# A router block and an experts block: logits turned first, lists copied on ScalarE, one gather and one fold moved across the block boundary

## The chip, the core and the metric

The kernel runs on one core of one Trainium2 chip. The time is the device time of that core in microseconds (us). TensorE, VectorE (DVE), ScalarE (ACT), GpSimd (POOL) and SyncE (SP) run their own instruction streams and meet by semaphores. SyncE computes nothing here; it issues DMAs, which 16 DMA engines carry out.

## What is computed

The reference runs two networks one after the other on a tensor x of 1024 tokens by 1024 features, all in fp32: a first block (modulated mixer of windowed attention and mLSTM, then a mixture of experts) and a second block of two layers (pooling and spatial gate, then dilated attention and short convolutions). The change lies in the mixture of experts and in a weight product that the second block's first layer wants ready:

```python
def expert_choice_ffn(h, w_router, w_gate, w_up, w_down):      # 16 experts, 1024 tokens
    cap = CAPACITY * N // N_EXPERTS                            # 128 tokens for each expert
    aff = jax.nn.softmax((h @ w_router).astype(f32), -1)
    gate, idx = lax.top_k(jnp.swapaxes(aff, 1, 2), cap)
    xg = h[bidx, idx]
    g = jnp.einsum('becd,edf->becf', xg, w_gate)
    u = jnp.einsum('becd,edf->becf', xg, w_up)
    y = jnp.einsum('becf,efd->becd', jax.nn.silu(g) * u, w_down) * gate[..., None]
    return jnp.zeros_like(h).at[bidx, idx].add(y)

# second block, even layer: z = h @ w_in; a is z's first quarter
pooled = trailing means of a minus a, in 4 groups of 256 features
mixed = jnp.einsum('bsgc,gcd->bsgd', pooled, pool_w)
```

The pooling runs over tokens and `pool_w` over features, so the kernel multiplies each group's 1024x256 slice of `w_in` with that group's `pool_w` beforehand. This product is called a fold. Three of the four groups are folded beside the router, each in two parts of 512 rows (parts P0 to P5), the fourth at the end of the experts.

## The kernel before

The program is a chain of blocks. A block holds one stream for each engine, and ends with a meeting of all of them. Semaphores of a block are taken from one of two sets in turn, and GpSimd clears the older set between blocks; a few semaphores are kept across blocks (`gathered`, `fold_stored`, `next_up_loaded`).

**`phase_router` (L2240 to L2538).** The products of x with the router's weights are in PSUM already (`router_z`). Its steps:

- TensorE first turns the shift column into rows (8 transposes, L2389), then the logits (2 transposes, L2394), which wait for ScalarE's copy of the products (L2453). ScalarE copies the shift rows (L2457) and then runs the exponential (L2459). VectorE does the rest of the softmax (L2490 to L2504).
- TensorE turns the affinities (L2400); VectorE copies them and finds the 128 best of each expert in 16 rounds of `max`, `max_index` and `match_replace` (L2516 to L2520), for both halves of the tokens at once.
- VectorE copies the lists: positions as floats, and both lists in reverse order (L2522 to L2524). TensorE turns all four (L2424, L2425), and VectorE merges the two halves into `slot_gate` and `slot_token` (L2528 to L2537).
- Beside it, in the order of `ORDER`, TensorE turns eight row blocks of x (R0 to R7, `turn_rows`), ScalarE scales them out of PSUM, GpSimd adds the shift (L2346), and SyncE stores them to `h2_rows` in memory (L2314). Between them stand the six fold parts: `turn_part` and `mix_part` on TensorE, `take_part` and `give_part` on ScalarE, `store_fold` on SyncE (L2319). ScalarE also casts the gate and up weights of expert 0 to their high parts (L2451) and GpSimd subtracts for their low parts (L2351).
- SyncE's last steps: it waits for all six mixes, loads `raw_up[1]` (L2333), whose buffer lies over fold part 0 and `w_mix`, and stores part 5.

**`phase_experts` (L2540 to L2898).** For each of 16 experts, every fp32 product is three matmuls on a high and a low part. GpSimd gathers the expert's 128 rows from `h2_rows` by `slot_token` (L2639), TensorE turns them (`turn`, L2676), then come `gate` (L2686 to L2690), `up` (L2699 to L2702), the turning of their product (L2710) and `down` (L2736 to L2741), one expert later. ScalarE casts weights and x to high parts (L2793, L2797), VectorE subtracts for the low parts (L2857, L2861), ScalarE weighs the result and GpSimd scatters it with an add (L2646). Raw weights have two buffers each. SyncE works through one list in order: it waits for both first gathers (L2614) and for the stored folds, loads `raw_down[1]`, the last fold's operands (L2615 to L2617), and then for each expert `load` (L2610), each released by the matmuls that have used the buffer's last contents.

Of the kernel before, what the change touches and what calls it, by code (L numbers as in the profile page):

```python
# [187 lines left out]
def build_program(nc, A, out):  # L188
    with ExitStack() as ctx:
# [2049 lines left out]

        def phase_router(router_z, first_turn):  # L2240
# [37 lines left out]
            first_fold_stored = sem("fold_first_stored")  # L2278
            top_done = sem("route_top_done")
            top_turned = sem("route_top_turned")  # L2280
            raw_loaded = sem("route_raw_loaded")
# [7 lines left out]
            turned_w = Arena(nc, ring_at + 2 * KT * P * 4 * 2)("fold_turned", [P, 2, 2, HALF])  # L2289
            fold_mem = Arena(nc, exp_raw_at["down", 1])  # L2290
            w_parts = [first_part] + [fold_mem(f"fold_part{g}", [P, KT, 2 * P]) for g in range(1, FOLDED)]
            assert fold_mem.at <= exp_mem.at
# [3 lines left out]

            def part_rows(i):
                return slice(i % 2 * (KT // 2), (i % 2 + 1) * (KT // 2))

            with nc.psum_tensor("route_fold", [P, 4, HALF], F32) as fold, nc.Block() as block:  # L2300
# [6 lines left out]
                @block.sync  # L2307
                def _(sp):
                    def load_part(g):
                        sp.dma_start(w_parts[g][:], even_w[:, :, g * 2 * P:(g + 1) * 2 * P]).then_inc(fold_loaded[g], 16)  # L2310

                    def store_rows(j):
                        sp.wait_ge(rows_shifted, 2 * j + 2)
                        sp.dma_start(h2_rows[j * P:(j + 1) * P, :], rows[j % SETS][:].rearrange("p a n -> p (a n)")).then_inc(stored[j % SETS], 16)  # L2314

                    def store_fold(i):
                        sp.wait_ge(fold_out, i + 1)
                        g = i // 2
                        sp.dma_start(fold_w[:, part_rows(i), g * 2 * P:(g + 1) * 2 * P], w_parts[g][:, part_rows(i), :]).then_inc(fold_stored if g else first_fold_stored, 16)  # L2319

                    load_part(1)
                    load_part(2)
                    for j in range(4):
                        store_rows(j)
                    sp.dma_start(exp_raw["down", 0][:], exp_src["down"][:, 0]).then_inc(raw_loaded, 16)
                    store_fold(0)
                    for j in range(4, BLOCKS):
                        store_rows(j)
                    for i in range(1, 5):
                        store_fold(i)  # L2330
                    sp.wait_ge(fold_mixed, 2 * FOLDED)
                    sp.wait_ge(first_fold_stored, 32)
                    sp.dma_start(exp_raw["up", 1][:], exp_src["up"][:, 1]).then_inc(next_up_loaded, 16)  # L2333
                    store_fold(5)
                    for u in range(SETS):
                        sp.wait_ge(stored[u], 16 * len(range(u, BLOCKS, SETS)))
                    sp.wait_ge(raw_loaded, 16)

                @block.gpsimd
                def _(pool):  # L2340
# [6 lines left out]
                    for n, w in enumerate(("gate", "up")):  # L2347
                        pool.wait_ge(hi_done, n + 1)
                        for part in range(4):
                            k = slice(part * EXP_SHAPES[w][1] // 4, (part + 1) * EXP_SHAPES[w][1] // 4)  # L2350
                            pool.tensor_tensor(exp_lo[w, 0][:, k], exp_raw[w, 0][:, k], exp_hi[w][:, k].bitcast(F32), ALU.subtract)  # L2351

                @block.tensor
                def _(pe):
# [32 lines left out]

                    for kt in range(KT):
# [3 lines left out]
                    pe.wait_ge(products_out, 1)  # L2392
                    for b in range(2):
                        ins = pe.transpose(logits[:, b * P:(b + 1) * P], products[:, b * P:(b + 1) * P], ident)  # L2394
                    ins.then_inc(logits_done, 1)
# [23 lines left out]
                    mix_part(5)  # L2419
                    pe.wait_ge(fold_out, 5)  # L2420
                    pe.wait_ge(top_done, 1)
# [7 lines left out]
                def _(act):  # L2429
# [51 lines left out]
                    give_part(5)  # L2481

                @block.vector
                def _(dve):
# [37 lines left out]
                    step(dve.tensor_copy(top_at_f[:], top_at[:]))  # L2522
                    step(dve.tensor_copy(top_back[:], top[:, ::-1]))
                    step(dve.tensor_copy(top_at_back[:], top_at[:, ::-1]))  # L2524
                    step.wait()
                    dve.sem_inc(top_done, 1)
# [10 lines left out]
                    step(dve.tensor_tensor(slot_token[:], apart[:], second[:, 1, :], ALU.add))  # L2537


        def phase_experts(first_rows, first_rows_loaded):  # L2540
# [4 lines left out]
            xg = mem("x_gathered", [P, 2, D])  # L2545
# [11 lines left out]
            gathered = [phases.keep(f"exp_gathered{u}") for u in range(2)]  # L2557
# [11 lines left out]
            half_down = sem("exp_half_down")  # L2569
            rows_copied = sem("exp_rows_copied")  # L2570
# [32 lines left out]
            with nc.psum_tensor("exp_turn", [P, 2, HALF], F32) as p_x, nc.psum_tensor("exp_gate", [P, 2, HALF], F32) as p_gu, \  # L2603
# [3 lines left out]
                def _(sp):  # L2607
# [4 lines left out]
                    for u in range(2):  # L2612
                        sp.wait_ge(gathered[u], 16)
# [21 lines left out]
                def _(pool):  # L2635
# [13 lines left out]
                    for e in range(4):  # L2649
# [20 lines left out]
                def _(pe):  # L2670
# [55 lines left out]
                    def down(e, halves_=range(2)):  # L2726
                        if 0 in halves_:
                            pe.wait_ge(f_hi_done, e + 1)
                            if e:
                                pe.wait_ge(y_out, e)  # L2730
                        for half in halves_:
# [11 lines left out]

                    turn(0)
# [39 lines left out]
                def _(act):  # L2784
# [26 lines left out]
                    hi("down", 0)  # L2811
                    hi_x(0)
# [2324 lines left out]
```

## Time and profile before

| | us |
|---|---|
| median of 3 runs | 3230.51 |
| lowest, highest | 3228.77, 3232.57 |
| the profiled execution | 3233.75 |
| its span in the trace | 3231.9 |
| TensorE busy (PE) | 3097.2 (96%) |
| VectorE, ScalarE, GpSimd busy | 1700.8, 1453.7, 1702.4 |
| DMA | 388.11 MB, 120 GB/s over the span |

In the trace the router's block lies from about 781 to 830 us and the experts' from there to about 1135. A row of a timeline gives start and duration in us, the engine, the line of the kernel, the operation, output<-input by the program's names, their shapes and the number of instructions merged; in brackets stands the idle time of the engine before it and what ended that. A row with xN above 1 runs from its start for its whole duration. `PEclk` is the granted clock of TensorE as a share of 2.4 GHz.

### The profile page before, as it was taken

To read this page: it belongs to the slowest core of one execution; us is meant where nothing else is said; L and a number is where in the kernel's file an instruction comes from. 1 tells how busy PE (TensorE), PEld (TensorE's weight loads), DVE (VectorE), ACT (ScalarE), POOL (GpSimd) and SP (SyncE) were. 2 spreads that over 40 slices of the span, in tenths; PEclk is the share of its full clock that TensorE was granted. 3 is DMA by queue.
4 is the path that set the end of the run, shared out by engine and by line. 5 is a ranking of instruction groups with operands and counts; after the bars stand their busy time and mean duration, and the time that the engine had idled before them with its cause. 6 is when DMAs were issued, how large, how long until landed. Compare 5 with 4: busy or idle time off the path is not lost. (4 is left out here: it accounts for less than half of the span.)

```text
span 3231.9 us, 43925 instructions
## 1 busy us (share of the span) xinstructions
PE 3097.2 (96%) x16268; PEld 2574.3 (80%) x16268; DVE 1700.8 (53%) x2449; ACT 1453.7 (45%) x2460; POOL 1702.4 (53%) x1112
## 2 busy tenths in 40 slices
PE   6989999979899989999999999999999999999998
PEld 4777887857688868788888788888888888888777
DVE  5366633855799776623523744444444444367545
ACT  5156322724577743333301545455455455333443
POOL 2331323044321249877643656556556556688886
PEclk8999999989899989999999999999999999999999
DMA  8230212175899952222422111111111111244543
GB/s 298 56 87 21 57 40 68 51 253 167 324 400 394 357 165 79 78 85 63 172 91 74 40 54 45 46 56 43 46 56 43 47 56 43 89 147 163 182 162 106
DMA packets 340339, 388.11 MB, mean 120 GB/s; under 512 B 29239, under 2 KB 297435, under 8 KB 333860
## 3 DMA queue, kind: packets, MB, share of 16 engines
q1 hardware_dynamic: 328222, 344.39, 31.7%
q0 software_dynamic: 4896, 16.78, 2.1%
q10 hardware_dynamic: 7014, 24.17, 1.9%
q8 instruction: 131, 2.15, 0.3%
q14 instruction: 76, 0.62, 0.1%
HBM read 313.73 MB, written 68.16 MB: 118 GB/s over the span
## 5 line engine op out<-in xcount | busy, mean ns | idle before, releaser
L3011 POOL TENSOR_TENSOR quarter_lo<-quarter_w_sums,quarter_hi 128x512 fp32r<-128x512 f32 x325 | 467.6, 1446 | 247.9 <-ACT quarter_hi L3005 245.1
L3011 POOL TENSOR_TENSOR quarter_lo<-quarter_raw,quarter_hi 128x512 fp32r<-128x512 f32 x244 | 356.2, 1460 | 277.7 <-ACT quarter_hi L3005 270.8
L3101 PE MATMUL odd_z<-odd_t_hi,quarter_hi 128*128 128x512 f32 x876 | 362.3, 414 | 4.0 <-POOL quarter_lo L3011 2.5
L3005 ACT CAST quarter_hi<-quarter_w_sums 128x512 fp32r<-128x512 f32 x325 | 202.4, 623 | 360.6 <-PE first_z L3103 172.8
L3101 PE MATMUL first_z<-odd_t_hi,quarter_hi 128*128 128x512 f32 x868 | 359.1, 414 | 4.1 <-ACT last_rows L3115 2.3
L3103 PE MATMUL odd_z<-odd_t_hi,quarter_lo 128*128 128x512 f32 x876 | 343.3, 392 | 0.0
L3102 PE MATMUL odd_z<-odd_t_lo,quarter_hi 128*128 128x512 f32 x876 | 341.9, 390 | 0.0
L3103 PE MATMUL first_z<-odd_t_hi,quarter_lo 128*128 128x512 f32 x868 | 340.4, 392 | 0.0
L3102 PE MATMUL first_z<-odd_t_lo,quarter_hi 128*128 128x512 f32 x868 | 338.8, 390 | 0.0
L3005 ACT CAST quarter_hi<-quarter_raw 128x512 fp32r<-128x512 f32 x244 | 151.6, 622 | 120.7 <-PE first_z L3103 55.8
L276 POOL TENSOR_TENSOR w_hi<-w_raw,zero_col 128x1024 fp32r<-128x1024 f32 x25 | 49.6, 1984 | 290.9 <-DMA w_raw<-in_w_in 98.1
L3101 PEld LDWEIGHTS odd_z<-odd_t_hi,quarter_hi 128*128 128x128 f32 x876 | 165.2, 189 | 35.9 <-POOL quarter_lo L3011 3.4
L3103 PEld LDWEIGHTS odd_z<-odd_t_hi,quarter_lo 128*128 128x128 f32 x876 | 164.6, 188 | 36.2
L3103 PEld LDWEIGHTS first_z<-odd_t_hi,quarter_lo 128*128 128x128 f32 x868 | 163.2, 188 | 35.9
L3101 PEld LDWEIGHTS first_z<-odd_t_hi,quarter_hi 128*128 128x128 f32 x868 | 163.7, 189 | 34.9 <-issue 5.5
L3102 PEld LDWEIGHTS odd_z<-odd_t_lo,quarter_hi 128*128 128x128 f32 x876 | 165.5, 189 | 30.0
L3102 PEld LDWEIGHTS first_z<-odd_t_lo,quarter_hi 128*128 128x128 f32 x868 | 164.0, 189 | 29.7
L4769 DVE SCALAR_TENSOR_TENSOR dil_biased<-const,odd_aux 128x128 f32<-128x128 f32 (+1 forms) x192 | 78.0, 406 | 192.7 <-PE odd_aux L4280 122.6
L3115 ACT ACTIVATE dil_set<-odd_z 128x512 f32<-128x512 f32 x112 | 90.8, 810 | 174.8 <-PE odd_z L3103 174.8
L3115 ACT ACTIVATE dil_set<-first_z 128x512 f32<-128x512 f32 x108 | 88.3, 817 | 166.6 <-PE first_z L3103 166.6
L4789 DVE COPY dil_p_t<-odd_aux 128x128 f32<-128x128 f32 (+1 forms) x192 | 67.7, 353 | 172.1 <-PE odd_aux L4297 150.7
L3018 POOL TENSOR_TENSOR quarter_w_sums<-quarter_raw 128x512 f32<-128x512 f32 x82 | 119.4, 1456 | 29.2 <-POOL quarter_lo L3011 13.4
(720 smaller groups left out, 7799.0 us busy)
## 6 DMA issues: line engine op xcount, KB each, us to landing
quarter_raw<-in_odd_w_in SPq DMA_DIRECT2D x224, 256.0 KB, 3.4
raw_gate<-in_w_gate SPq DMA_DIRECT2D x16, 2048.0 KB, 15.5
raw_up<-in_w_up SPq DMA_DIRECT2D x16, 2048.0 KB, 15.0
raw_down<-in_w_down SPq DMA_DIRECT2D x16, 2048.0 KB, 14.9
quarter_raw<-in_even_w_in SPq DMA_DIRECT2D x64, 256.0 KB, 3.2
start_w_mod<-in_w_mod SPq DMA_DIRECT2D x11, 1024.0 KB, 10.8
w_raw<-in_w_in SPq DMA_DIRECT2D x16, 512.0 KB, 3.8
mix_w_early<-in_w_mod SPq DMA_DIRECT2D x8, 1024.0 KB, 12.0
```

The lines of the kernel that those rows point to most:

```text
L276: pool.tensor_tensor(w_hi[:, u], w_raw[:, u], zero_col[:, 0:1].to_broadcast([P, KT * P]).rearrange("p (k n) -> p k n", k=KT), ALU.add).the ...
L3005: act.copy(self.home(n)[0][:], self.source(m, i)).then_inc(self.hi_done, 1)
L3011: pool.tensor_tensor(lo[:], self.source(m, i), hi[:].bitcast(F32), ALU.subtract).then_inc(self.split, 1)
L3018: pool.tensor_tensor(sums[:, 0], a21, a22, ALU.add).then_inc(self.added, 1)
L3101: pe.matmul(to, w_hi[:, kt], t_hi[:, kt], start=(begins and kt == 0), stop=False, skip_group_check=True)
L3102: pe.matmul(to, w_hi[:, kt], t_lo[:, kt], start=False, stop=False, skip_group_check=True)
L3103: ins = pe.matmul(to, w_lo[:, kt], t_hi[:, kt], start=False, stop=(kt == KT // 2 - 1), skip_group_check=True)
L3115: act.activation(to[t][half], self.bank(m, i, banks, to), ACT.Copy, scale=scale).then_inc(self.copied, 1)
L4769: dve.scalar_tensor_tensor(out=biased[:, u % 2, 0:w], in0=dist, scalar=cst("slopes")[:, g * C_SLOTS + h:g * C_SLOTS + h + 1], in1=score[:, ...
L4789: dve.tensor_copy(p_t[:, u % 2, 0:w], turned[:, 0:w]).then_inc(free, 1)
```

## The change

The logits are turned ahead of the shift. The three copies of the lists go from VectorE to ScalarE, with a semaphore `top_found` from VectorE and a count of three on `top_done`. GpSimd issues the gather for expert 0 at the end of the router's block, behind its subtractions, a wait for all stored rows and a new semaphore `slots_known`; the tile `x_gathered` and its semaphores are therefore made outside both phases. The mix of fold part 5 leaves the router's block and is done by TensorE at the start of the experts' block, into `p_y`, ahead of `turn(0)`; ScalarE copies it out behind the cast of down(0), and SyncE stores it. The load of `raw_up[1]` moves with it: SyncE issues it behind gather 0 and that mix, and stores part 5 next. Nothing of the work is left out.

```diff
@@ -2237,6 +2237,18 @@
+        xg_mem = Arena(nc, exp_mem.at)
+        xg = xg_mem("x_gathered", [P, 2, D])
+        xg_end = xg_mem.at
+        gathered = [phases.keep(f"exp_gathered{u}") for u in range(2)]
+        turned_w = Arena(nc, ring_at + 2 * KT * P * 4 * 2)("fold_turned", [P, 2, 2, HALF])
+        fold_parts_mem = Arena(nc, exp_raw_at["down", 1])
+        w_parts = [first_part] + [fold_parts_mem(f"fold_part{g}", [P, KT, 2 * P]) for g in range(1, FOLDED)]
+        assert fold_parts_mem.at <= exp_mem.at
...
+        def part_rows(i):
+            return slice(i % 2 * (KT // 2), (i % 2 + 1) * (KT // 2))
...
         def phase_router(router_z, first_turn):
@@ -2276,8 +2288,10 @@
             first_fold_stored = sem("fold_first_stored")
+            top_found = sem("route_top_found")
             top_done = sem("route_top_done")
             top_turned = sem("route_top_turned")
+            slots_known = sem("route_slots_known")
             raw_loaded = sem("route_raw_loaded")
@@ -2286,16 +2300,9 @@
             wide = [P, BLOCKS, N_EXPERTS]
-            turned_w = Arena(nc, ring_at + 2 * KT * P * 4 * 2)("fold_turned", [P, 2, 2, HALF])
-            fold_mem = Arena(nc, exp_raw_at["down", 1])
-            w_parts = [first_part] + [fold_mem(f"fold_part{g}", [P, KT, 2 * P]) for g in range(1, FOLDED)]
-            assert fold_mem.at <= exp_mem.at
             ORDER = "R0 R1 P0 P1 R2 R3 R4 P2 R5 R6 R7 P3 P4 P5".split()
...
             FOLD_AT = [ORDER.index(f"P{i}") for i in range(2 * FOLDED)]
...
-            def part_rows(i):
-                return slice(i % 2 * (KT // 2), (i % 2 + 1) * (KT // 2))
@@ -2326,12 +2333,9 @@
                         store_rows(j)
-                    for i in range(1, 5):
+                    for i in range(1, 2 * FOLDED - 1):
                         store_fold(i)
-                    sp.wait_ge(fold_mixed, 2 * FOLDED)
                     sp.wait_ge(first_fold_stored, 32)
-                    sp.dma_start(exp_raw["up", 1][:], exp_src["up"][:, 1]).then_inc(next_up_loaded, 16)
-                    store_fold(5)
                     for u in range(SETS):
@@ -2349,6 +2353,11 @@
                             pool.tensor_tensor(exp_lo[w, 0][:, k], exp_raw[w, 0][:, k], exp_hi[w][:, k].bitcast(F32), ALU.subtract)
+                    for u in range(SETS):
+                        pool.wait_ge(stored[u], 16 * len(range(u, BLOCKS, SETS)))
+                    pool.wait_ge(slots_known, 1)
+                    pool.indirect_dma_start(xg[:, 0, :], None, h2_rows, bass.IndirectOffsetOnAxis(ap=slot_token[:, 0:1], axis=0),
+                                            bounds_check=SEQ - 1).then_inc(gathered[0], 16)
@@ -2385,14 +2394,14 @@
+                    pe.wait_ge(products_out, 1)
+                    for b in range(2):
+                        ins = pe.transpose(logits[:, b * P:(b + 1) * P], products[:, b * P:(b + 1) * P], ident)
+                    ins.then_inc(logits_done, 1)
                     for kt in range(KT):
...
                             ins.then_inc(shift_turned, 1)
-                    pe.wait_ge(products_out, 1)
-                    for b in range(2):
-                        ins = pe.transpose(logits[:, b * P:(b + 1) * P], products[:, b * P:(b + 1) * P], ident)
-                    ins.then_inc(logits_done, 1)
                     turn_rows(0)
@@ -2416,9 +2425,8 @@
                     mix_part(4)
-                    mix_part(5)
                     pe.wait_ge(fold_out, 5)
-                    pe.wait_ge(top_done, 1)
+                    pe.wait_ge(top_done, 3)
@@ -2478,7 +2486,10 @@
                     give_part(4)
-                    give_part(5)
+                    act.wait_ge(top_found, 1)
+                    act.copy(top_back[:], top[:, ::-1]).then_inc(top_done, 1)
+                    act.copy(top_at_f[:], top_at[:]).then_inc(top_done, 1)
+                    act.copy(top_at_back[:], top_at[:, ::-1]).then_inc(top_done, 1)
@@ -2519,11 +2530,7 @@
                         step.wait()
-                    step(dve.tensor_copy(top_at_f[:], top_at[:]))
-                    step(dve.tensor_copy(top_back[:], top[:, ::-1]))
-                    step(dve.tensor_copy(top_at_back[:], top_at[:, ::-1]))
-                    step.wait()
-                    dve.sem_inc(top_done, 1)
+                    dve.sem_inc(top_found, 1)
                     dve.wait_ge(top_turned, 1)
@@ -2535,6 +2542,8 @@
                     step(dve.tensor_tensor(slot_token[:], apart[:], second[:, 1, :], ALU.add))
+                    step.wait()
+                    dve.sem_inc(slots_known, 1)
@@ -2542,7 +2551,7 @@
             FK, shapes, raw, w_hi_, w_lo_ = FFK, EXP_SHAPES, exp_raw, exp_hi, exp_lo
-            xg = mem("x_gathered", [P, 2, D])
+            mem.at = xg_end
             x_hi = mem("x_hi", [P, 2, KT, P], F32R)
@@ -2554,7 +2563,6 @@
             used = {w: sem(f"exp_{w}_used") for w in shapes}
-            gathered = [phases.keep(f"exp_gathered{u}") for u in range(2)]
             turned = sem("exp_turned")
@@ -2567,6 +2575,8 @@
             half_down = sem("exp_half_down")
+            part_mixed = sem("fold_rest_mixed")
+            part_out = sem("fold_rest_out")
             rows_copied = sem("exp_rows_copied")
@@ -2609,8 +2619,12 @@
-                    for u in range(2):
-                        sp.wait_ge(gathered[u], 16)
+                    sp.wait_ge(gathered[0], 16)
+                    sp.wait_ge(part_mixed, 1)
+                    sp.dma_start(raw["up", 1][:], exp_src["up"][:, 1]).then_inc(next_up_loaded, 16)
+                    sp.wait_ge(part_out, 1)
+                    sp.dma_start(fold_w[:, part_rows(5), 4 * P:6 * P], w_parts[2][:, part_rows(5), :]).then_inc(fold_stored, 16)
+                    sp.wait_ge(gathered[1], 16)
                     sp.wait_ge(fold_stored, 16 * 2 * (FOLDED - 1))
@@ -2646,7 +2660,7 @@
-                    for e in range(4):
+                    for e in range(1, 4):
                         gather(e)
@@ -2728,6 +2742,8 @@
                                 pe.wait_ge(y_out, e)
+                            else:
+                                pe.wait_ge(part_out, 1)
                         for half in halves_:
@@ -2741,6 +2757,11 @@
+                    for kt in range(KT // 2):
+                        for c in range(2):
+                            ins = pe.matmul(p_y[:, kt // 2, kt % 2 * 2 * P:(kt % 2 + 1) * 2 * P], turned_w[:, 1, c, kt * P:(kt + 1) * P],
+                                            w_mix[:, 4 + c, :], start=(c == 0), stop=(c == 1))
+                    ins.then_inc(part_mixed, 1)
                     turn(0)
@@ -2809,6 +2830,8 @@
                     hi("down", 0)
+                    act.wait_ge(part_mixed, 1)
+                    act.copy(w_parts[2][:, part_rows(5), :].rearrange("p (a k) n -> p a (k n)", a=2), p_y[:]).then_inc(part_out, 1)
                     hi_x(0)
```

## Rows read from the trace of the kernel before

**Rows 1.** Stretches: us, busy us (instructions) of PE, PEld, DVE, ACT, POOL; PEclk, DMA share, GB/s

```profile
821.00:831.00 10.00, 2.03 (x9) 1.78 (x8) 6.97 (x17) 1.85 (x2) 5.37 (x3) 0.66 0.81 266
831.00:842.00 11.00, 5.08 (x15) 4.08 (x16) 5.72 (x3) 5.15 (x4) 4.82 (x3) 0.50 0.55 159
842.00:890.00 48.00, 46.90 (x217) 38.88 (x216) 35.95 (x21) 32.21 (x23) 6.56 (x3) 0.97 0.99 377
890.00:1110.00 220.00, 220.00 (x1044) 183.67 (x1043) 199.62 (x111) 173.66 (x124) 48.83 (x24) 1.00 1.02 396
```

**Rows 2.** Timeline of SyncE's DMA queue: loads around the boundary, and two gate loads

```profile
821.21 0.35 SPq L2333 DMA_DIRECT2D raw_up<-in_w_up  x1
...
838.82 0.35 SPq L2615 DMA_DIRECT2D raw_down<-in_w_down  x1
...
839.70 3.71 SPq L2617 DMA_DIRECT2D fold_last_mix<-in_even_pool_w  x1
...
860.56 0.33 SPq L2610 DMA_DIRECT2D raw_gate<-in_w_gate  x1
...
1073.33 0.33 SPq L2610 DMA_DIRECT2D raw_gate<-in_w_gate  x1
```

**Rows 3.** DMA issues at 822, 860 and 1073 us; last number: us to landing

```profile
fold_w<-fold_part SPq DMA_DIRECT2D x1, 512.0 KB, 10.3
...
raw_gate<-in_w_gate SPq DMA_DIRECT2D x1, 2048.0 KB, 8.1
...
raw_gate<-in_w_gate SPq DMA_DIRECT2D x1, 2048.0 KB, 21.0
```

**Rows 4.** Timelines of VectorE and TensorE late in the experts: down(14)

```profile
1108.25 4.49 DVE L2857 TENSOR_TENSOR lo_down<-raw_down,hi_down 128x2048 fp32r<-128x2048 f32 x2 [0.40 <-ACT hi_down L2793]
...
1115.41 0.39 PE L2736 MATMUL exp_y<-hi_down,f_hi 128*128 128x512 f32 x1
```

**Rows 5.** Timeline of VectorE: the lists' copies and the merge

```profile
822.85 3.60 DVE L2522 CAST aff_top_at_f<-aff_top_at 48x128 f32<-48x128 uint32 x1
...
826.51 0.21 DVE L2524 CAST aff_top_at_back<-aff_top_at 48x128 f32<-48x128 uint32 x1
828.82 0.17 DVE L2528 COPY aff_second<-route_fold 128x16 f32<-128x16 f32 x1 [2.10 <-PE route_fold L2425]
...
829.69 0.18 DVE L2537 TENSOR_TENSOR slot_token<-aff_apart,aff_second 128x16 uint32<-128x16 f32 x1
```

**Rows 6.** Timeline of GpSimd: last subtractions, gathers 0 and 2

```profile
817.11 9.26 POOL L2351 TENSOR_TENSOR lo_up<-raw_up,hi_up 128x1024 fp32r<-128x1024 f32 x4
831.19 1.24 POOL L2639 DMA_INDIRECT x_gathered<-h_rows,slot_token  x1 [4.82 <-issue]
...
838.56 1.01 POOL L2639 DMA_INDIRECT x_gathered<-h_rows,slot_token  x1 [3.26 <-PE exp_turn L2676]
```

**Rows 7.** Timeline of TensorE: start of the router's block, folds 4 and 5, expert 0

```profile
781.38 1.94 PE L2389 MATMUL route_fold<-const,mod 128*128 128x128 f32 x8 [0.58 <-PEq L2054]
783.12 0.46 PE L2394 MATMUL route_fold<-const,aff_products 128*128 128x128 f32 x2
...
814.10 7.07 PE L2384 MATMUL route_fold<-fold_w_mix,fold_turned 128*128 128x256 f32 x32
...
835.82 1.97 PE L2676 MATMUL exp_turn<-const,x_gathered 128*128 128x128 f32 x8 [7.04 <-DMA x_gathered<-h_rows,slot_token]
838.89 0.80 PE L2686 MATMUL exp_gate<-hi_gate,x_hi 128*128 128x512 f32 x1 [1.10 <-ACT x_hi L2797]
...
845.37 2.00 PE L2690 MATMUL exp_gate<-hi_gate,x_lo 128*128 128x512 f32 x8
847.20 0.39 PE L2699 MATMUL exp_gate<-hi_up,x_hi 128*128 128x512 f32 x1
```

**Rows 8.** Timeline of ScalarE at the start of the router's block

```profile
783.15 1.06 ACT L2457 COPY h_shift_rows<-route_fold 128x512 f32<-128x512 f32 x2
784.98 0.31 ACT L2459 ACTIVATE aff<-aff 128x128 f32<-128x128 f32 x1 [0.77 <-DVE aff L2496]
```

## The prediction

> **What bounds the kernel now.** I read the page first, then the stretch tables, and then each engine's timeline around the edited code, because the edit touches 60 us of a 3232 us span. Two facts come out of the tables. From 890 to 1110 us, inside the experts, TensorE is busy 220.00 of 220.00 us, and the DMA engines are busy too, at a share of 1.02 and 396 GB/s [rows 1]. So two resources are full at once, and the question is which of them ends an expert.
>
> The queue of SyncE answers it. The gate load of expert 3 is issued at 860.56 and that of expert 15 at 1073.33 [rows 2]; both are released by TensorE, so TensorE needs (1073.33 - 860.56)/12 = 17.73 us for an expert. The first of them lands 8.1 us after its issue, the second 21.0 us after [rows 3]. They land at 868.7 and 1094.3, so the DMA engines need 18.8 us for an expert. The transfers fall behind TensorE by about 1.1 us with every expert, and TensorE does not notice it, because each buffer is asked for early. What is left of that cover at the end can be read off: the low part of down(14) is ready at 1108.25 + 4.49 = 1112.74, and the first matmul that needs its second half runs at 1115.41 [rows 4]. The cover is 2.7 us.
>
> Ahead of the experts lies the serial chain that the change shortens. The lists of the router end on VectorE with a cast of a 48x128 tile that took 3.60 us, while the same cast took 0.21 us right behind it [rows 5]. GpSimd's four subtractions run from 817.11 to 826.37 [rows 6], and the long cast ends at 826.45, just behind them: VectorE waited for GpSimd's SBUF access. Then come TensorE's turning of the lists (VectorE idle 2.10 us), 1.05 us of small steps to 829.87, the block's end, GpSimd's gather at 831.19, and TensorE's first transposes for expert 0 at 835.82 [rows 5 to 7]. The first gate projection starts at 838.89, behind a wait of 1.10 us for the high part of x, and runs at half clock: TensorE's granted clock was 0.50 from 831 to 842 (1.2 GHz) and 1.00 later [rows 1, 7].
>
> **Part 1, logits turned first.** TensorE enters the block at 781.38 and turned the shift for 1.94 us before it came to the logits at 783.12 [rows 7]. Now only ScalarE's short copy of the products lies ahead of them; I put their start at 781.8. VectorE's chain to the exponential would be about 1.1 us earlier. But ScalarE has the two copies of the shift rows (783.15, 1.06 us for both) ahead of the exponential (784.98) [rows 8], and those now wait for transposes that start 0.9 us later. These end at about 782.3 + 1.6 to 1.9, and the exponential comes at about 784.5 to 784.8. I take a gain of 0.35 us; bounds 0 and 1.1.
>
> **Part 2, lists copied by ScalarE.** ScalarE is free then: its last copy of a fold part leaves the block, and a 128x128 exponential took 0.31 us [rows 8]. Three copies back to back take about 0.75 us (bounds 0.6 and 1.2). They replace 826.72 - 822.85 = 3.87 us on VectorE [rows 5]. Gain 3.1 us. Chain: index search done at 822.47, lists at 823.3, turned at 825.2 (about 1.9 us as now), small steps to 826.3. Two of these steps read two SBUF tiles; GpSimd is then at its last subtraction (to about 826.0), so up to 0.3 us is added: slots known at about 826.55 instead of 829.9.
> The Trainium skill says the same of the wait: the "GPSIMD Engine Reference", section Key points, has GpSimd sharing its SBUF interfaces with VectorE, in conflict with a two-port mode or with two SBUF inputs. By it the cast goes, and the 0.3 us of the two-input steps stays; the trace agrees as to the cast (3.60 against 0.21 us).
>
> **Part 3, first gather in the router's block.** From a semaphore to the start of a gather GpSimd took 0.77 us (TensorE's turn ends at 837.79, the gather starts at 838.56), and the instruction lasts 1.24 us [rows 6, 7]. So it starts at 827.3 and ends at 828.55. All engines now wait for GpSimd at the block's end: the experts' block opens at about 829.05 where it did at about 830.16. The rows arrive 4.63 us after the start (835.82 - 831.19 [rows 6, 7]), at 831.9. That is 3.9 us earlier, and it is not what is late next.
>
> **Part 4, sixth fold in the experts' block.** It is 16 matmuls, half of 7.07 us, which ran at full clock at 817.6 while TensorE had nothing else [rows 7]: they cost nothing there. Now they stand ahead of turn(0), on the path. TensorE is idle from about 817.3 except for 1.9 us of small matmuls; over the same kind of pause its clock fell in the trace (0.66 mean from 821 to 831, 0.50 to 842) and had not risen 6.2 us after 835.82 [rows 1, 7]. Bounds of the 16 matmuls: 3.55 us at full clock, 7.1 us at half. I take 5.7 us, begun at half and finished at full. They end at M = 829.05 + 5.7 = 834.75 (bounds 832.6 and 836.15). Then turn(0) at full clock, half of 1.97, and the 1.10 us wait for x: gate(0) starts at 836.9. It has 24 matmuls and took 847.20 - 838.89 = 8.3 us; its last eight took 847.20 - 845.37 = 1.83 us [rows 7], at full clock, so 24 of them need 5.5 us, so up(0) starts at 842.4 instead of 847.20: **TensorE is 4.8 us ahead** (bounds 3.4 and 7.0). ScalarE's copy of the fold part, 128x1024, is as long as its two 128x512 copies (1.06 us [rows 8]) and lies beside turn(0), which takes as long.
> The Trainium skill speaks against this part: "TensorE: Matmul & The Clock Gate", section Loop structure matters more than you think, has the loop nest decide whether matmuls run warm, an idle wait in it bringing the half clock back. By it the fold is moved from a warm place to a cold one, 7.1 instead of 3.55 us; by its first half alone, that work warms what follows, gate(0) gains 2.8 us. My sum holds both.
>
> **Part 5, what is queued behind it.** This is the part that decides. The load of up(1) was issued at 821.21 [rows 2], while the router's lists were still being sorted. Its buffer overlays the fold's operands, so it now waits for gather 0 and the sixth fold: M = 834.75, 13.5 us later. The store of the sixth part follows it, as before, and landed 10.3 us after an issue that was 1.04 us behind the load's [rows 3]: it lands at M + 11.3 = 846.1. Behind that store SyncE holds down(1), the last fold's operands and then gate(2), issued at 838.82 before [rows 2]. Up(1) itself, ahead of the store in the queue, arrives in time. But the bytes are the same, in less time. Unused DMA time from 821 to 890, against the full rate of 396 GB/s [rows 1]: before, 10(1 - 266/396) + 11(1 - 159/396) + 48(1 - 377/396) = 3.3 + 6.6 + 2.3 = 12.2 us. After, 821 to 834.75 holds two gathers alone (about 1.1 MB, 2.8 us): 11.0 us unused; 834.75 to 848 holds 2.6 MB and one gather, 8.0 us: 5.3 us unused. Behind that the queue is never empty. 11.0 + 5.3 - 12.2 = **4.1 us later for every transfer from about expert 4 on** (bounds by M: 1.9 and 5.5).
>
> **The sum.** At the end of the experts TensorE can be ahead of the old time by no more than cover minus lateness: 2.7 - 4.1 = -1.4. The 4.8 us are spent waiting for weights, and 1.4 us more. Behind the experts the scatters and row loads move with it, and the later stages start from there. The profiled execution took 3233.75 us for a span of 3231.9; it becomes 3235.15. The median of the three runs is 3230.51, 3.2 us below that execution; the same difference on it gives 3231.9.
>
> **Rivals.**
> A, forecast: transfers take over as the bound late in the experts: +1.4 us, 3231.9; by the bounds of M and 1 us on the unused time, 3229 to 3235.
> B: the DMA engines give more than 396 GB/s when more is queued, or fetch earlier than I reckon. Then TensorE keeps its lead: -4.8 us, 3225.7; with the fold at full clock -7.0 us, 3223.5. For it: in all of 890 to 1110 TensorE never waited. Against it: the landing time grows steadily from 8.1 to 21.0 us, which is a queue that is full, with a share of 1.02.
> C, slower: SyncE serves one list in order. It holds at the fold's store, and the issue of the last fold's weights took 3.71 us by itself [rows 2]; gate(2) would then be issued at about 850.5, 8 us after TensorE has freed its buffer. If the DMA engines run dry in that hold, at the worst for the whole 3.7 us, and the fold ran at half clock (M = 836.15, 5.5 us late), then 2.7 - 9.2 = 6.5 us slower: 3237.0. It decides from the point at which the lateness passes 9.2 us. Against it: 3.4 MB are queued ahead of gate(2) by then.
> D: the chain of lists does not get shorter, because GpSimd is late at its gather and opens the experts' block at 830.2 after all. M is 835.9, the lateness 5.3 us: +2.6 us, 3233.1.
> The Trainium skill's "DMA: Bandwidth & Descriptors", section Issuing engines are not separate DMA queues, has DMAs of all issuers interleave on the same 16 engines. It speaks against B: the gather on GpSimd's queue and SyncE's loads draw on one rate, as the share of 1.02 with both in flight shows.
>
> **How the numbers follow.** Chances: A 0.55, B 0.27, C 0.13, D 0.05. A measurement of this kernel tells about 0.2% (6.5 us) from no change. A and D lie within it, and B's own value too; B's part beyond 6.5 us is the fold at full clock, 0.12. C's 6.5 us stands on the line, and I count it as slower with 0.13. Faster 0.12, same 0.75, slower 0.13. The range leaves out the fast end of B and the slow end of C: 3225.4 to 3237.0.
>
> **What would show it.** In the profile after: ScalarE's three copies at about 822.5 and lists turned by 825.3; gather 0 starting at 827 to 828; 16 fold matmuls from 829 on, longer than 3.6 us; up(0) 4 to 5 us ahead of 847.20. Then the landing time of the gate load of expert 3 near 16 to 18 us instead of 8.1, and, late in the experts, TensorE idle behind casts that wait for raw weights, which the trace of before has nowhere. The forecast is wrong if TensorE stays without a wait up to 1110 (B), or if the DMA engines show a gap around 850 (C).

## The result

| | before | after |
|---|---|---|
| median of 20 runs, us | 3231.14 | 3236.99 |
| lowest, highest | 3227.57, 3234.82 | 3233.47, 3241.36 |
| span of the profiled execution | 3231.9 | 3234.8 |

The ratio is 1.0021, 95% interval 1.0015 to 1.0027: slower by 5.85 us between the medians and 6.8 us by the ratio, with an interval that lies clear of 1. The forecast was 1.4 us, called no change with 0.75. The measured 3236.99 us is the number of rival C (3237.0), which had 0.13; the part on why the prediction was wrong says how much of that is C's mechanism.

Two profiles do not enter the router's block at the same time. I align them on ScalarE's copy of the products, the block's first work: 781.36 before, 779.35 after. An "aligned" time is counted from there. gate(e), up(e) and down(e) are the three products of expert e, or the load of their weights; up(0) as a time is the first matmul of that product.

The chain of the lists got shorter, as planned. After, timelines of VectorE and GpSimd:

```profile
819.04 0.68 DVE L2529 FIND_INDEX8 aff_top_at<-aff_top,aff_left 48x8 uint32<-48x512 f32 x1
822.54 0.17 DVE L2535 COPY aff_second<-route_fold 128x16 f32<-128x16 f32 x1 [2.82 <-PE route_fold L2433]
...
823.41 0.17 DVE L2544 TENSOR_TENSOR slot_token<-aff_apart,aff_second 128x16 uint32<-128x16 f32 x1
829.57 0.17 DVE L2887 CAST exp_half_row<-slot_token 128x2 f32<-128x2 uint32 x1 [5.99 <-PEq L2307]
```

```profile
824.64 1.24 POOL L2359 DMA_INDIRECT x_gathered<-h_rows,slot_token  x1 [1.41 <-DVEq L2546]
830.47 1.04 POOL L2653 DMA_INDIRECT x_gathered<-h_rows,slot_token  x1 [4.59 <-issue]
```

The slots are known 4.3 us sooner (823.58 - 779.35 = 44.2, against 829.87 - 781.36 = 48.5 [rows 5]). GpSimd has issued the gather at 825.88. But VectorE's next instruction, the first of the experts' block, comes at 829.57, after 5.99 us in which no engine computed; GpSimd's issue of the gather was the only instruction. The gather took 4.6 us from its start to land, here as before: 824.64 + 4.6 = 829.2. The block opened right behind the landing. TensorE and SyncE from there:

```profile
829.57 6.34 PE L2762 MATMUL exp_y<-fold_w_mix,fold_turned 128*128 128x256 f32 x16 [7.07 <-PEq L2307]
835.75 1.05 PE L2690 MATMUL exp_turn<-const,x_gathered 128*128 128x128 f32 x8
```

```profile
836.00 0.35 SPq L2624 DMA_DIRECT2D raw_up<-in_w_up  x1
836.99 0.36 SPq L2626 DMA_DIRECT2D fold_w<-fold_part  x1
848.40 0.34 SPq L2629 DMA_DIRECT2D raw_down<-in_w_down  x1
...
849.28 3.40 SPq L2631 DMA_DIRECT2D fold_last_mix<-in_even_pool_w  x1
852.72 2.59 SPq L2620 DMA_DIRECT2D raw_gate<-in_w_gate  x1
```

The fold takes 6.34 us in its cold place (granted clock 0.50 in the ten microseconds up to 831, below). The up load follows at 836.00, where it stood at 821.21 [rows 2]. SyncE then stands 11 us for the fold's store, and gate(2) is issued at 852.7; TensorE had freed its buffer at about 843.7. Stretches of the kernel after (columns as in [rows 1]), and who waited from 850 to 1145 us (us in total, times, longest):

```profile
821.00:831.00 10.00, 2.93 (x12) 2.57 (x12) 1.35 (x10) 1.45 (x1) 4.00 (x3) 0.50 0.17 52
831.00:842.00 11.00, 9.87 (x40) 8.01 (x39) 5.72 (x3) 5.46 (x5) 1.52 (x2) 0.82 0.61 207
842.00:890.00 48.00, 44.59 (x204) 36.26 (x203) 33.00 (x19) 31.63 (x23) 5.79 (x3) 0.96 0.95 366
...
844.00:851.00 7.00, 6.01 (x31) 4.96 (x29) 4.04 (x3) 4.88 (x5) 0.21 (x1) 1.00 0.62 192
...
950.00:1110.00 160.00, 158.06 (x746) 130.97 (x745) 139.68 (x80) 121.14 (x88) 36.19 (x16) 1.00 1.02 396
```

```profile
ACT hi_up L2814 <- DMA raw_up<-in_w_up: 21.5, 11, 2.8
...
ACT hi_down L2814 <- DMA raw_down<-in_w_down: 14.4, 10, 2.9
...
ACT hi_gate L2814 <- DMA raw_gate<-in_w_gate: 11.1, 10, 8.4
...
PE exp_gate L2700 <- ACT x_hi L2818: 3.4, 2, 2.3
```

From 821 to 831 the DMA engines moved 52 GB/s where they had moved 266 [rows 1]. From 844 to 851, at the end of SyncE's stand for the store, they moved 192 GB/s, and nothing at all from 848 to 849. In the same aligned stretch before it was 399:

```profile
846.00:853.00 7.00, 7.00 (x34) 5.81 (x34) 2.37 (x2) 4.21 (x3) 0.00 (x0) 1.00 1.07 399
```

ScalarE waits 47 us for raw weights, where it had waited 7.7 us in all, and TensorE now loses time in two stretches in which it had lost little or none: it is busy 44.59 of 48 us where it was 46.90, and 158.06 of 160 us where it never stopped [rows 1]. The gate load of expert 15 is issued at 1074.04 and lands 26.9 us later (21.0 before [rows 3]):

```profile
raw_gate<-in_w_gate SPq DMA_DIRECT2D x1, 2048.0 KB, 26.9
```

It lands at 1100.9, aligned 321.6 against 313.0: the transfers are 8.6 us late.

### The profile page after: what moved, and what is told of

Its sections match the earlier page's. It is cut to its first block and busy times, and to the rows that moved or that the text cites. A ratio compares the mean times of both kernels' runs of the same rounds, so it can differ in the third digit from the quotient of the medians.

```text
span 3234.8 us, 43929 instructions
## 1 busy us (share of the span) xinstructions
PE 3095.9 (96%) x16268; PEld 2571.8 (80%) x16268; DVE 1694.8 (52%) x2446; ACT 1454.5 (45%) x2463; POOL 1708.7 (53%) x1112
## 5 line engine op out<-in xcount | busy, mean ns | idle before, releaser
L2660 POOL DMA_INDIRECT ffn_rows<-expert_y,slot_token x14 | 37.1, 2647 | 196.3 <-ACT expert_y L2824 186.0
```

The source lines that it names most:

```text
L2660: pool.indirect_dma_start(ffn_rows, bass.IndirectOffsetOnAxis(ap=slot_token[:, e:e + 1], axis=0), y[:, e % 2, :], None, bounds_check=SEQ - ...
```

## The experiments

All ratios are against the kernel before, with 95% intervals. Every ratio here lies within 0.2% of 1, so most of them only bound the effect, and the reading rests on the aligned times of one trace for each kernel, in the table behind the last run. "End of the experts" there is TensorE's first matmul of the last fold. Two warnings go with these times. The stages behind the table differ by up to 3.4 us between executions. And in four kernels whose chain of VectorE up to the slots is the same code, the slots are known at 48.5 (before), 47.6, 47.6 and 47.9: the trace of before is the latest of the four, so a difference of less than 0.9 us from it says nothing by itself.

**Gather back.** The changed kernel, with gather 0 again in the experts' block:

```diff
...
-                    pool.wait_ge(slots_known, 1)
-                    pool.indirect_dma_start(xg[:, 0, :], ...).then_inc(gathered[0], 16)
...
-                    for e in range(1, 4):
+                    for e in range(4):
                         gather(e)
```

> The changed kernel with the gather for expert 0 back in the experts' block. Theory 1: in the changed kernel the router's block does not end when GpSimd has issued the gather but when its rows have landed (slots known at 823.58, rows landed at 829.2, block opened at 829.5), and the late sixth fold and up load then make every transfer late, up to the end of the experts. Then here the experts' block opens about 0.3 us after the slots are known, the fold ends about 5.9 us sooner than in the changed kernel, the transfers are about 5.9 us less late, and the time is that of the kernel before within 1.5 us (ratio 0.9995 to 1.0005). Rival 1a: another engine holds the block's end; it still opens 5 to 6 us after the slots are known, and the ratio stays near 1.002. Rival 1b: the fold in its cold place is the whole loss; the block opens early, but the ratio stays above 1.001.

Measured: ratio 1.0003 (0.9994 to 1.0013). The block opens right behind the slots (timeline of VectorE):

```profile
823.80 0.17 DVE L2539 TENSOR_TENSOR slot_token<-aff_apart,aff_second 128x16 uint32<-128x16 f32 x1
824.42 0.17 DVE L2882 CAST exp_half_row<-slot_token 128x2 f32<-128x2 uint32 x1 [0.44 <-PEq L2307]
```

Rival 1a falls: nothing else held the block. 1b as I put it falls too; the fold is in its cold place here as well (5.64 us against 6.34), and up(0) starts 7.6 us ahead of before.

**First two parts alone.** The kernel before with the logits' order and the lists' copies of the change:

```diff
+                    pe.wait_ge(products_out, 1)
+                    ... transposes of the logits, ahead of those of the shift
...
-                    step(dve.tensor_copy(top_at_f[:], top_at[:]))   # and the two others
+                    act.copy(top_at_f[:], top_at[:]).then_inc(top_done, 1)
```

> The kernel before with the first two parts of the change alone: logits turned ahead of the shift, lists copied by ScalarE; gather, sixth fold and up load where they were. Theory 1: slots known 4.2 us sooner, block, gathers, down(1) and gate(0) move with it, and the load of up(1) stays in the router's block, so the transfers are not late: 4 us faster (ratio 0.9988). Rival 2: the transfers bound the end of the experts in any case, and a lead of TensorE is worth at most the cover of 2.7 us: ratio 0.9992 or nearer to 1.

Measured: 0.9993 (0.9984 to 1.0002), which holds the value of either theory; the trace decides. The slots came 3.5 us sooner, up(0) and the end of the experts 2.7 us, the even layer's first matmul 1.6 us. Gather 0 landed 5.85 us after its start instead of 4.6, beside the up load. The size agrees with rival 2, but not its reason: TensorE was not held by weights (the transfers landed 1.8 us sooner, and with the cover of 2.7 us they would have let 4.5 us through).

**Fold and up load moved alone.**

```diff
-                    mix_part(5)
...
-                    sp.dma_start(exp_raw["up", 1][:], ...)          # both now in phase_experts,
-                    store_fold(5)                                   # as in the change
```

> The kernel before with the sixth fold and the up load moved to the experts' block alone, gather and lists as before. Theory 1: block opens at 830.2, fold ends at about 836.4, up(0) starts at about 844 (3 us sooner than before), transfers 5.8 us late, less 2.7 us of cover: 3 us slower (ratio 1.0010), with ScalarE waiting for raw weights from about expert 3 on. Rival 2b: TensorE's path alone decides, and the 3 us at up(0) stay a gain: ratio 0.9990.

Measured: 1.0012 (1.0003 to 1.0021), end of the experts 3.6 us late though up(0) was 4.3 us ahead. As theory 1 says, and against rival 2b. It leaves open whether the cold fold or the late load did it.

**Gather moved alone.**

```diff
...
+                    pool.wait_ge(slots_known, 1)
+                    pool.indirect_dma_start(xg[:, 0, :], ...).then_inc(gathered[0], 16)
...
```

> The kernel before with the gather for expert 0 moved into the router's block alone. Theory 1: slots known at 829.9, gather at 830.7, landed at 835.3, and only then the block opens; the cast of down(0) on ScalarE and gather 1 start 5.3 us later than before; high part of x behind that cast, gate(0) 1.5 us later than before, down(1) 3.7 us later: 1.5 us slower (ratio 1.0005), and the gap between slots known and the block's opening is 5.5 us. Rival 1a: the block opens 2.4 us after the slots are known, gate(0) comes at the old time or 0.3 us sooner: ratio 1.0000 to 0.9997.

Measured: 1.0004 (0.9995 to 1.0013), which alone tells nothing. The timelines of VectorE and GpSimd do:

```profile
826.60 0.17 DVE L2548 TENSOR_TENSOR slot_token<-aff_apart,aff_second 128x16 uint32<-128x16 f32 x1
832.56 0.17 DVE L2876 CAST exp_half_row<-slot_token 128x2 f32<-128x2 uint32 x1 [5.79 <-PEq L2306]
```

```profile
827.83 1.24 POOL L2361 DMA_INDIRECT x_gathered<-h_rows,slot_token  x1 [4.56 <-DVEq L2550]
```

The stall of 5.8 us came with the gather and nothing else of the change. Rival 1a asked for 2.4 us. The rest of the expectation missed: gate(0) came 0.5 us later than before, not 1.5, and the end of the experts did not move.

**Few gathers, before and after.** To take load from the DMA engines without touching the edited code, both kernels leave out the gathers for experts 4 to 15, which then compute on old rows:

```diff
-                        if e + 4 < E:
-                            gather(e + 4)
...
-                        pe.wait_ge(gathered[e % 2], 16 * (e // 2 + 1))
+                        pe.wait_ge(gathered[e % 2], 16 * (min(e // 2, 1) + 1))
```

> The kernel before without the gathers for experts 4 to 15; these experts compute on the rows of experts 2 and 3 again, so that part of the work is left out and the result changed. It is the partner of the next run. Each gather is about 1.4 us of the DMA engines, so they need 17.4 us for an expert instead of 18.8, less than TensorE's 17.73. Both theories: TensorE was never held by weights here, so the end of the experts does not move; at most 1 us is saved where the scatters and the row loads end them: ratio 0.9996 to 1.0000, landing times that stop growing.

> The changed kernel without the gathers for experts 4 to 15, which is left out as in the run before it. Theory 1, late transfers are the whole loss: they catch up, TensorE is not held, and its lead of 1.7 us at up(0) reaches the end: 1 to 2 us faster than the partner run (ratio to the kernel before 0.9991 to 0.9997). Rival 1b, the fold in its cold place or another wait of TensorE is the loss: the distance to the partner stays near that of the full kernels, 5 to 7 us slower (ratio 1.0015 or more).

Measured: 0.9998 (0.9989 to 1.0007) and 1.0014 (1.0005 to 1.0023). This is a miss for theory 1 as it stood. The transfers did catch up (both kernels' last gate load lands 12.5 us after its issue, and ScalarE no longer waits for weights late), and still the end of the experts was 3.6 us behind the partner's. The waits of the second kernel name the place; the loss lies in expert 2, and from 890 to 1110 us TensorE was busy throughout:

```profile
ACT hi_gate L2812 <- DMA raw_gate<-in_w_gate: 8.3, 1, 8.3
...
PE exp_gate L2698 <- ACT x_hi L2816: 3.3, 2, 2.2
```

ScalarE works in order: while it waits 8.3 us for gate(2), the high part of x stands behind it, and TensorE behind that. So there are two losses of TensorE, one early and one late, of which the later hides the earlier.

**Late up load, warm fold.** The two first parts, the fold in the router's block, but the up load and the store of part 5 issued behind gather 0:

```diff
-                    sp.dma_start(exp_raw["up", 1][:], ...).then_inc(next_up_loaded, 16)
-                    store_fold(5)
...
+                    sp.wait_ge(gathered[0], 16)
+                    sp.dma_start(raw["up", 1][:], ...).then_inc(next_up_loaded, 16)
```

> The kernel with logits turned first and lists copied by ScalarE, with the sixth fold left warm in the router's block, but the load of up(1) and the store of fold part 5 issued in the experts' block behind gather 0, as in the changed kernel. It takes the late load without the cold fold. Theory 1: up(0) starts as in the kernel with the two first parts alone (2.7 us ahead of before), but transfers are late by about 2 us against before, as with the gather back in its block (ratio 1.0003): the late load costs about 3 us against 0.9993, ratio 1.0001 to 1.0005. Rival 1b, the cold fold costs the time: ratio stays at 0.9993.

Measured: 0.9999 (0.9990 to 1.0009), transfers 2.6 us late, end of the experts 0.1 us ahead of before, with 5.5 us of lead at up(0) where 2.7 were expected. The ratio does not exclude rival 1b's 0.9993; the trace does: the lead is gone at the end, so the late load costs this without any cold fold.

**No wait for the gathers.**

```diff
-                    for u in range(2):
-                        sp.wait_ge(gathered[u], 16)
```

> The kernel with logits turned first and lists copied by ScalarE (0.9993), and SyncE's loads of down(1) and of the last fold no longer held until both first gathers have landed, only until the folds are stored. Theory 1, the DMA engines bound the end of the experts: down(1) is issued about 3.3 us sooner, every later transfer lands up to 3 us sooner, and of the 3.5 us by which the lists are ready sooner all reach the even layer instead of 1.6: ratio 0.9986 to 0.9990. Rival 3: gather 1 now shares the DMA engines with down(1), or TensorE's lead of 2.7 us is all there is: ratio 0.9991 to 0.9995.

Measured: 0.9995 (0.9985 to 1.0004), the end at 342.0 as with the two parts alone (341.8), though down(1) was issued 3.1 us sooner than there. Rival 3: TensorE's lead at up(0), 2.5 us, was all there was.

**gate(2) first,** in the changed kernel and in the one with the gather back:

```diff
+                    load("gate", 2)
                     sp.wait_ge(gathered[1], 16)
                     sp.wait_ge(fold_stored, 16 * 2 * (FOLDED - 1))
```

> The changed kernel with the load of gate(2) ahead of SyncE's wait for the folds' stores, of down(1) and of the last fold's loads. In the changed kernel TensorE leads by 1.7 us at up(0) and is 2.7 us behind at the fourth gate, because gate(2) is issued at 852.7, 9 us after its buffer is free, and its cast waits 8.4 us. Theory 4: SyncE's order makes that early stall and leaves the DMA engines idle from 844 to 848. Then the stall of 4.4 us goes here, the fourth gate comes 1.7 us sooner than before, all transfers land about 4 us sooner than in the changed kernel, and the end is 4 us sooner: ratio 1.0009 (1.0006 to 1.0012). Rival: down(1) and the last fold's loads, now later, hold the experts instead; or the number of late bytes alone counts: ratio 1.0018 or more.

> The changed kernel with the gather for expert 0 back in the experts' block and the load of gate(2) first, as in the first run of this set. With the gather back TensorE led by 7.6 us at up(0), lost 3.8 us at the third expert, and the end was 0.5 us ahead of before. Theory 4: with gate(2) issued at 838 the stall goes and the transfers land 4 us sooner, 1.9 us ahead of before; the end is 1.9 + 2.7 = 4.6 us ahead: ratio 0.9988. Rival as above: ratio 1.0000 or more.

Measured: 1.0016 (1.0007 to 1.0025) and 0.9987 (0.9978 to 0.9996). In the first the early stall is gone (TensorE busy 46.90 of 48 us from 842 to 890, as before), so is the gap of the DMA engines, and the end of the experts comes 3.5 us sooner than in the changed kernel. The stretch that had moved 192 GB/s there:

```profile
843.00:850.00 7.00, 6.33 (x33) 5.20 (x31) 3.72 (x3) 4.83 (x4) 0.00 (x0) 1.00 1.03 395
```

That is the 4 us of theory 4 in the trace; the ratio, with an interval of 0.0018, does not separate 1.0009 from 1.0018. The second is as expected, 0.9988, and faster than the kernel before: this is the change without the step that failed and with the load order mended.

**Warm TensorE.** 14 unread matmuls in the wait for gather 0, on the two first parts:

```diff
+                    for n in range(14):
+                        pe.matmul(p_y[:, n % 2, :], w_hi_["gate"][:, n % KT, 0:P], w_hi_["gate"][:, n % KT, :], start=True, stop=True)
                     turn(0)
```

> The kernel with logits turned first and lists copied by ScalarE (0.9993), with 14 matmuls more whose results nobody reads, at the start of the experts' block, where TensorE waits 7 us for gather 0. If TensorE's clock at gate(0) is what the cold stretch costs, gate(0) runs at full clock and up(0) starts 2.5 us sooner; the cover of 2.7 us and transfers 1.8 us ahead let 4.5 us through: end of the experts 4.5 us ahead of before instead of 2.7, ratio 0.9988. Rival: it is all lost at the scatters and row loads behind the experts: ratio 0.9993.

> The same with 14 matmuls for warmth, and SyncE's loads of down(1) and of the last fold not held for the first gathers. If the transfers bound the end of the warm kernel, this one lets the whole lead of 5.2 us through: ratio 0.9985 to 0.9988, and faster than the warm kernel by up to 1 us. If the scatters behind the experts bound it, both are alike.

Measured: 0.9987 (0.9978 to 0.9996) and 0.9990 (0.9981 to 0.9999). The first kernel's added matmuls, and the stretch of gate(0):

```profile
826.03 5.63 PE L2746 MATMUL exp_y<-hi_gate 128*128 128x512 f32 x14 [2.15 <-PEq L2301]
```

```profile
834.00:842.00 8.00, 6.90 (x32) 5.58 (x31) 1.23 (x1) 3.15 (x4) 1.01 (x1) 1.00 0.73 279
```

Gate(0) ran at a granted clock of 1.00, where the two parts alone had 0.58 over the same 8 us. Up(0) started 2.9 us sooner than without the matmuls, and the end of the experts was 5.6 us (4.5 expected) and 6.6 us ahead of before. Both beat the kernel before; between them the runs do not decide.

| aligned us | slots known | block opens | up(0) | gate load 15 lands | end of experts | even layer starts |
|---|---|---|---|---|---|---|
| before | 48.5 | 48.8 | 65.8 | 313.0 | 344.5 | 356.3 |
| after | 44.2 | 50.2 | 64.2 | 321.6 | 350.5 | 362.5 |
| gather back | 44.2 | 44.7 | 58.2 | 315.1 | 344.0 | 358.5 |
| first two parts | 45.0 | 45.3 | 63.1 | 311.2 | 341.8 | 354.7 |
| fold moved alone | 47.6 | 48.0 | 61.5 | | 348.0 | 362.1 |
| gather moved alone | 47.6 | 53.4 | 65.7 | | 344.4 | 357.6 |
| before, few gathers | 47.9 | 48.2 | 65.0 | 303.6 | 343.7 | 356.7 |
| after, few gathers | 44.2 | 50.2 | 64.2 | 307.2 | 347.2 | 360.6 |
| late up load | 44.3 | 44.7 | 60.3 | 315.6 | 344.4 | 356.2 |
| no wait for the gathers | 45.0 | 45.4 | 63.4 | | 342.0 | 354.2 |
| after, gate(2) first | 44.2 | 50.2 | 64.3 | 318.1 | 347.0 | 359.6 |
| gather back, gate(2) first | 44.2 | 44.7 | 58.1 | 311.3 | 340.1 | 355.1 |
| warm | 45.0 | 45.4 | 60.3 | | 338.9 | 350.9 |
| warm, no wait for the gathers | 44.1 | 44.5 | 59.3 | 307.6 | 337.9 | 351.4 |

An empty field means that the trace gives no landing time.

## Why the prediction was wrong

**What bounds (right).** The sum was: lateness of the transfers less a cover of 2.7 us. With the measured lateness it gives the end of the experts in the five kernels whose late experts waited for transfers and whose trace has a landing time. After: 8.6 - 2.7 = 5.9, measured 5.97. Gather back: 2.1 - 2.7 = -0.6, measured -0.5. Late up load: 2.6 - 2.7, measured -0.1. gate(2) first: 5.1 - 2.7 = 2.4, measured 2.5; with the gather back -1.7 - 2.7 = -4.4, measured -4.4. The same without the trace of before: in these five the end comes 28.8 to 28.9 us behind the landing of gate load 15, and in the kernel before 31.5, 2.7 us more. Where the transfers did not bind, TensorE's lead at up(0) reached the end instead: 2.7 and 2.7 us with the first two parts, 5.5 and 5.6 with the warm kernel.

**Part 1 (cannot be told from its forecast).** 0.35 us forecast. Against the trace of before the affinities were turned 1.1 us and the exponential started 0.8 us sooner. But the exponential starts at 2.85 here, at 3.62 before, and at 2.74, 2.74 and 3.00 in the three other kernels that turn the shift first (fold moved alone, gather moved alone, before with few gathers). So most of the 1.1 us is the spread of the trace of before. The last index search ends at 40.4 here and at 40.6 in the two kernels with one step moved alone: 0.2 us.

**Part 2 (right).** 3.1 us forecast; from the last index search to the slots 3.9 us instead of 7.05, a gain of 3.2. The three copies cost 0.7 us on ScalarE. The 0.3 us set aside for the steps with two inputs did not come: from the merge's first copy to the slots it took 1.04 us, as before (1.05).

**Part 3 (the step that failed).** I let the experts' block open when GpSimd had issued the gather, at aligned 47.7. It opened at 50.2, when the rows had landed. I had taken the issue's 1.24 us for all that GpSimd must finish; no row of before showed a block that ends behind a gather. D came nearest with a late opening (830.2, aligned 48.8), but gave it another cause, which did not occur: the slots were known early and the gather started at 45.3.

**Part 4 (size).** The fold took 6.34 us, 5.7 forecast, inside the bounds; with the gather back and the block open at 44.7 it took 5.64 us. With part 3 its end M was 56.6 aligned instead of 53.4, and the lead at up(0) 1.7 us instead of 4.8.

**Part 5 (size, and a hold taken for harmless).** 4.1 us of lateness forecast, 8.6 measured. The later M adds 3.2: 2.5 from part 3, 0.6 from part 4. The other error is SyncE's order. The prediction says that behind 848 "the queue is never empty"; it ran empty before SyncE had done standing for the fold's store. 7(1 - 192/396) = 3.6 us of DMA time went unused from 844 to 851, none in the kernel with gate(2) first (395 GB/s), and moving that load took 3.5 us of lateness away. I had written that hold down as rival C, with a gap around 850 as its sign, and called it unlikely because 3.4 MB were queued. It also starved expert 2: from up(0) to the release of expert 4's gate load TensorE needed 4.4 us more than before. I had checked whether up(1) came in time, and not gate(2). The two errors add up to 6.7 us, and only 4.5 are missing: without the hold the lateness was 5.1 us, where part 5 with the true M gives 7.3, so it reckoned 2.2 us too much elsewhere. Counted as in part 5, unused DMA time over the same 69 us was 12.2 us before (326 GB/s) and 19.3 after (285 GB/s). That is 7.1 of the 8.6 us; where the other 1.5 come from is open.

**Sum.** 1.4 forecast, and 4.5 us more of lateness: 5.9 us at the end of the experts; 6.25 at the even layer. The measured time agrees with it. That it is also C's number is half luck: C had the hold right (3.7 us at the worst), but took the rest from a fold at half clock and knew nothing of the gather; its lateness is 9.2 us, the measured one 8.6.

## What to carry to other kernels

Before a step moves across a block's end, ask what the end will then wait for: an issued transfer may count as unfinished, as the gather did here. Where transfer and compute are both full, write down the landing time of one load in each round; if it grows, expect a byte that is moved behind an idle stretch of the DMA engines to come back as lateness at the end, less the cover that is left. And when a load is moved in an in-order queue, follow every load behind it to its first reader, and ask what the DMA engines have left to do while the queue waits.

## What the runs showed of the hardware

A block whose last GpSimd instruction was a gather ended when its rows had landed: VectorE was idle for 5.79 to 5.99 us there in all four kernels that have it (the gather took 4.6 us from start to landing), and for 0.32 to 0.44 us in the ten that do not. By what signal the end waits was not tried.

The issue of a 256 KB load (`fold_last_mix`) right behind 3 MB of loads held SyncE for 3.40 us in the kernel after and 3.71 us before [rows 2], and the next one, in the kernel after, for 2.59 us; most other issues took 0.33 to 0.36 us. In the kernel after the DMA engines had moved nothing in the microsecond before, so no older backlog held it there; the cause was not tried.

Fourteen matmuls without a use, in a wait of 7 us, gave 2.9 us back: the granted clock from 834 to 842 us was 0.58 without them, and the first gate projection ran at 1.00 with them.
